# A two-block transformer kernel: the fourth sum of each pair of down weights, made by an adding DMA before, made by VectorE

## The reference, cut to what matters

```python
def conv_gated_ffn(x, w_up, w_gate, conv_w, conv_b, w_down):
    u = x @ w_up
    g = causal_dwconv(x @ w_gate, conv_w, conv_b)
    return (jax.nn.silu(g) * u) @ w_down

def swiglu(h, w_gate, w_up, w_down):
    return (jax.nn.silu(h @ w_gate) * (h @ w_up)) @ w_down
```

## Time and profile before

| what | value |
|---|---|
| median of 3 runs | 2264.41 us (2259.07 to 2270.99) |
| the profiled execution's own time | 2263.4 us |
| its span in the profile | 2261.8 us |
| TensorE's granted clock, mean | 0.997 of full |
| VectorE, ScalarE, GpSimd busy | 73%, 53%, 32% of the span |
| transfers | 350.75 MB, 155 GB/s in the mean |
| queue of GpSimd's transfers | 92.29 MB, 19.3% of 16 engines |

### The profile page before, as it was taken

The page is one execution under the profiler, slowest core; times in us unless marked ns, Lnnn a source line. Parts: engine busy times, 40 slices in busy tenths (PEclk is TensorE's granted clock), DMA queues, the critical chain, the costliest instruction groups (busy, mean ns, idle before and its releaser), DMA issues.

```text
span 2261.8 us, 37043 instructions
## 1 busy us (share of the span) xinstructions
PE 2195.7 (97%) x13094; PEld 1886.0 (83%) x13094; DVE 1644.0 (73%) x2447; ACT 1199.5 (53%) x2126; POOL 720.7 (32%) x482
## 2 busy tenths in 40 slices
PE   8999999999999999999999999999899999999998
PEld 6767898888888787899987899988778768899986
DVE  6966656678744345766698888888658972899898
ACT  6665444456655545443465644456645674444475
POOL 6944444321236535322102322221112343311101
PEclk9999999999999999999999999999999999999999
DMA  6636465675458864332264256695354593223364
GB/s 207 197 117 246 147 154 140 152 209 192 159 198 170 193 237 139 118 102 97 98 214 163 75 139 145 144 244 189 136 190 150 123 148 93 101 96 110 102 223 144
DMA packets 117497, 350.75 MB, mean 155 GB/s; under 512 B 12496, under 2 KB 12496, under 8 KB 117328
## 3 DMA queue, kind: packets, MB, share of 16 engines
q1 hardware_dynamic: 76320, 242.91, 32.0%
q0 software_dynamic: 36928, 92.29, 19.3%
q10 hardware_dynamic: 4144, 14.16, 1.9%
HBM read 338.76 MB, written 94.37 MB: 191 GB/s over the span
## 4 chain that ended last, share of the span: by engine, by line
PE 75%; DVE 10%; ACT 6%; DMA 5%; issue 2%; POOL 1%; DVEq 0%; SPq 0%; ACTq 0%; POOLq 0%
PE banks L953 9%; PE banks L955 8%; PE banks L954 8%; PE banks L1162 5%; PE banks L1164 5%; PE banks L1163 5%; PE banks L1251 4%; PE banks L1253 4%; PE banks L1252 4%; DMA raw<-ws 4%; PE banks L1296 3%; PE banks L1298 3%; PE banks L1297 3%; PE banks L986 2%; PE banks L988 2%
## 5 line engine op out<-in xcount | busy, mean ns | idle before, releaser
L1849 ACT ACTIVATE wH<-raw 128x1024 fp32r<-128x1024 f32 x363 | 380.9, 1052 | 419.3 <-DMA raw<-ws 138.5
L690 POOL TENSOR_TENSOR wL<-raw,wH 128x1024 fp32r<-128x1024 f32 x110 | 282.4, 2572 | 447.5 <-ACT wH L1849 444.0
L953 PE MATMUL banks<-xH,wH 128*128 128x512 f32 (+1 forms) x1080 | 413.4, 383 | 11.4 <-DVE xL L2587 7.4
L954 PE MATMUL banks<-xL,wH 128*128 128x512 f32 (+1 forms) x1080 | 407.8, 378 | 0.0
L955 PE MATMUL banks<-xH,wL 128*128 128x512 f32 (+1 forms) x1080 | 407.7, 377 | 0.0
L953 PEld LDWEIGHTS banks<-xH,wH 128*128 128x128 f32 x1080 | 203.7, 189 | 57.0 <-DVE wL L2592 8.5
L955 PEld LDWEIGHTS banks<-xH,wL 128*128 128x128 f32 x1080 | 203.6, 188 | 38.0
L954 PEld LDWEIGHTS banks<-xL,wH 128*128 128x128 f32 x1080 | 203.9, 189 | 35.4
L853 POOL TENSOR_TENSOR wL<-raw,wH 128x1024 fp32r<-128x1024 f32 x36 | 100.6, 2796 | 187.0 <-ACT wH L1849 187.0
L1162 PE MATMUL banks<-wH,mixXH 128*128 128x512 f32 x312 | 122.8, 393 | 12.0 <-DVE mixXL L2996 7.0
L1163 PE MATMUL banks<-wH,mixXL 128*128 128x512 f32 x312 | 121.5, 389 | 0.0
(11 more groups left out here) (416 smaller groups left out, 6230.4 us busy)
## 6 DMA issues: line engine op xcount, KB each, us to landing
raw<-ws SPq DMA_DIRECT2D x327, 512.0 KB, 3.3
raw<-sums SPq DMA_DIRECT2D x44, 512.0 KB, 4.2
sums<-ws POOLq DMA_DIRECT2D x20, 1024.0 KB, 6.4
firsts<-ws POOLq DMA_DIRECT2D x44, 256.0 KB, 5.0
sums<-firsts POOLq DMA_DIRECT2D x44, 256.0 KB, 5.8
thirds<-ws POOLq DMA_DIRECT2D x44, 256.0 KB, 6.3
sums<-sums POOLq DMA_DIRECT2D x44, 256.0 KB, 5.7
raw<-ws SPq DMA_DIRECT2D x44, 256.0 KB, 3.3
```

Of the source, the lines that this page charges most:

```text
L690: pool.tensor_tensor(wL[:, j, :], raw[:, j, :], fp(wH[:, j, :]), ALU.subtract).then_inc(low_ready, 1)
L953: pe.matmul(bank, wH[:, slot, cols], rh, start=start, stop=False)
L954: pe.matmul(bank, wH[:, slot, cols], rl, start=False, stop=False)
L1849: act.activation(high_slot(c)[:, 0:w], raw_slot(c)[:, 0:w], ACT.Copy).then_inc(high_ready, 1)
```

## The change: what it does, and the diff

The adding transfer of the fourth sum is removed from GpSimd's list, in every place where it stood, with the semaphore `fourth_added` and SyncE's wait for it. The row of `sums` that SyncE loads into the slot of an odd chunk now has the bare quarter in its left half. VectorE adds the right half to the left in the slot (`fourth_sum` in VectorE's list), once the load has landed, and ScalarE's high part of an odd chunk waits for that (`fourth_there`, semaphore `fourth_made`). The addition for pair 0 stands in the last tile of gate-and-up, ahead of `part_sums(0)`; that for pair 1 right after `low_of_chunk(0)`; that for pair p + 1 between the low parts of h of pair p and `low_of_chunk(2p + 1)`. The step-wise sums have one step less.

```diff
                     elif i < FT:
                         sp_e.wait_ge(second_added, 16 * n + 16)
-                        sp_e.wait_ge(fourth_added, 16 * n + 16)
                         sp_e.dma_start(to, sums[n]).then_inc(loaded(c), 16)
...
-            def fourth_sum(inst, j, t=0):
-
-                n = NP * inst + j
-                pool.wait_ge(second_added, t * 16 + (16 * n + 16))
-                if n:
-                    pool.wait_ge(fourth_added, t * 16 + 16 * n)
-                pool.sem_inc(adding, 1)
-                pool.dma_start(half_of(sums, t + n, 0), half_of(sums, t + n, 1), accum_op=ALU.add)\
-                    .then_inc(fourth_added, 16)
-
...
                 if 1 <= j <= NP:
                     second_sum(inst, j - 1)
-                if j >= 2:
-                    fourth_sum(inst, j - 2)
...
                     first_sum(inst, 2, t)
-                    fourth_sum(inst, 1, t)
                     low(cp + 9, t)
...
+                def fourth_there(j):
+                    act.wait_ge(fourth_made, NP * inst + j + 1)
+
...
                     if last:
+                        fourth_there(0)
                         high(d0 + 1)
...
                     def chunk(i):
+                        if i < FT and i % 2:
+                            fourth_there(i // 2)
                         high(d0 + i, w=S if i == Y_AT[NP - 1] else D)
...
                     if last:
+                        fourth_sum(0)
                         part_sums(0)
                         low_of_chunk(1)
...
+                def fourth_sum(j):
+                    c = d0 + 2 * j + 1
+                    dve.wait_ge(loaded(c), 16 * LOADED[c])
+                    quarters = raw_slot(c)
+                    dve.tensor_tensor(quarters[:, 0:S], quarters[:, 0:S], quarters[:, S:D], ALU.add).then_inc(fourth_made, 1)
...
                     low_of_chunk(0)
+                    fourth_sum(1)
...
                         parts(p, 2 * p)
+                        if p + 1 < NP:
+                            fourth_sum(p + 1)
                         low_of_chunk(2 * p + 1)
```

More of the change, by code:

```diff
@@ L366, in build_block @@
         third_added = sem("third_added")
-        fourth_added = sem("fourth_added")
+        fourth_made = sem("fourth_made")
         adding = sem("adding")
@@ L830, in plain_splits @@
                         first_sum(inst, 0, t)
-                        fourth_sum(inst, -1, t)
                         low_of_last_sum(u, 1, t)
@@ L838, in plain_splits @@
                     first_sum(inst, count - 1)
-                    fourth_sum(inst, count - 2)
                     low_of_last_sum(u, 1, count - 1)
@@ L844, in plain_splits @@
                         first_sum(inst, j)
-                        fourth_sum(inst, j - 1)
                         second_sum(inst, j)
                         third_sum(inst, j)
-                    fourth_sum(inst, NP - 1)
                     return
@@ L874, in plain_splits @@
                 first_sum(inst, 1)
-                fourth_sum(inst, 0)
                 low(cp + 5)
@@ L890, in plain_splits @@
                         first_sum(inst, j + 1)
-                    fourth_sum(inst, j)
             def down_parts(inst):
@@ L920, in _ @@
                 if inst == 1:
-                    for n in range(NP + 2):
+                    for n in range(NP + 1):
                         split(begun // SLOTS, begun % SLOTS)
```

## The result

The changed kernel takes **2270.55 us** (median of 20 runs, 2266.96 to 2274.58), the kernel before, run beside it, 2264.14 (20 runs): a ratio of **1.0027, 95% interval 1.0019 to 1.0035**. That is inside the range and within 0.5%, so "same" was right, and 5 us above the forecast of 2265.4; the rise is 6.4 us where 2.0 was forecast. The profiled execution took 2269.18 us with a span of 2267.5.

The account below looks back on a forecast made before the run. TensorE was taken as the bound, busy 2195.7 of 2261.8 us. Down stages +5.0 less 3.0 in gate-and-up gave +2.0 on the profiled 2263.4: 2265.4 us, range 2256 to 2274.

Parts of the forecast that it names:

- Pairs of 4.94 us, additions of 0.69: Down stages: a VectorE addition takes 0.69 us and lengthens its pair from 4.34 to 4.94, under TensorE's 5.44.
- Starts of instances 0 and 1, +1.0 each: Start of these down stages: the first two additions delay TensorE by 0.44 and 0.60 us, with no wait for a load.
- Instance 3, a new wait at the head of VectorE's queue, +1.6: Down stage start: the second addition waits for chunk 3, costing 1.35 us; the third, for chunk 5, another 0.3.
- Instance 2, +1.4 between -2.5 and +3.3: Down stage start: +3.3 us with the same landings, -2.5 with landings as in instance 3; a third of the way taken.
- From the third pair on the additions cost nothing: Down stages: VectorE's lead still grows by 0.50 us a pair instead of 1.10, so later additions stay covered.
- rival 3: Inside the pairs: additions lengthened beside GpSimd's tensor work make VectorE the bound, 16 us more, 2281; chance 0.05.
- Gate-and-up, -2.5 and -0.5: Gate-and-up of instances 2 and 0: less adding traffic shortens TensorE's waits of 5.7 and 1.8 us by 2.5 and 0.5.
- Rival 1, no relief: Other adding transfers remain in flight, no load comes sooner, down stage starts cost 8.1 us: 2271.5; chance 0.20.

Follow-up runs that it names:

- combines_off: Changed kernel with GpSimd's three additions of kept parts in each down stage left out of the computation: 2264.75 us, ratio 0.9996.
- traffic_back: Changed kernel plus a fourth adding transfer per pair, issued by GpSimd into a scratch tensor that nothing reads: 2279.38 us, ratio 1.0075.
- split_late_first: Changed kernel, adding transfers back in instances 1 and 3, pair 1's addition behind its low parts, instance 0's kept-part additions on VectorE: 2263.20 us, ratio 0.9987.
- gpsimd_sum: Changed kernel with the 44 additions of quarters made by GpSimd in the down stage instead of VectorE: 2298.95 us, ratio 1.0149.
- before_combine: Kernel before, adding transfers kept, with the three additions of kept parts in each down stage on VectorE instead of GpSimd: 2261.60 us, ratio 0.9998.
- late_first: Changed kernel with only pair 1's addition moved, from ahead of its part sums to behind its low parts: 2271.19 us, ratio 1.0028.

## Why the prediction was right, and where it wasn't

- **Pairs of 4.94 us, additions of 0.69.** Right: 44 of 685 ns in the mean, and successive pairs begin 4.94 apart, here in DVE's timeline:

```profile
519.38 0.68 DVE L2952 TENSOR_TENSOR raw<-raw 128x512 f32<-128x512 f32 x1
...
524.32 0.69 DVE L2952 TENSOR_TENSOR raw<-raw 128x512 f32<-128x512 f32 x1
```

- **Starts of instances 0 and 1, +1.0 each.** Right: TensorE's first wait went from 0.63 to 1.04 in both, the third from 0.50 and 0.53 to 1.12 and 1.10. No wait for a landing in either.
- **Instance 3, a new wait at the head of VectorE's queue, +1.6.** Right: 1.1 us of waiting for chunk 3 were forecast, and the stage grew by 1.8. In answer to the earlier trace rows (DVE, then PE):

```profile
2155.43 0.69 DVE L2952 TENSOR_TENSOR raw<-raw 128x512 f32<-128x512 f32 x1 [1.05 <-DMA raw<-sums]
...
2159.38 0.50 PE L1142 MATMUL banks<-wH,mixXH 128*128 128x512 f32 x1 [1.25 <-DVE mixXL L2994]
```

- **Instance 2, +1.4 between -2.5 and +3.3.** It was +2.1, by waits and clock together. VectorE waits 3.86 us for chunk 3 at its second addition and 1.63 for chunk 5 at its third, against the earlier trace rows:

```profile
1499.72 0.69 DVE L2952 TENSOR_TENSOR raw<-raw 128x512 f32<-128x512 f32 x1 [3.86 <-DMA raw<-sums]
...
1503.67 0.50 PE L1142 MATMUL banks<-wH,mixXH 128*128 128x512 f32 x1 [4.06 <-DVE mixXL L2994]
...
1505.25 0.69 DVE L2952 TENSOR_TENSOR raw<-raw 128x512 f32<-128x512 f32 x1 [1.63 <-DMA raw<-sums]
```

  The waits at the start sum to hardly more than before (5.28 us start to start against 5.00), but now one of them is 4.45 us long, and half clock follows it.
- **"From the third pair on the additions cost nothing."** This is the step that failed. It holds for the pairs, to whose end I followed it: no matmul waits there. But a lead that grows by 0.50 instead of 1.10 is 0.60 x 9 = 5.4 us shorter when the pairs are over, and behind the pairs stand GpSimd's three operations. I had the price of such contention in rival 3 and dismissed it with "within the pairs GpSimd has no tensor work to do"; true, and the wrong place to look. The row of 7.0 us shown above, TensorE's wait for VectorE near the end of all four stages, said already before the change that VectorE's time counts there. The contention cost 2.7 and 4.3 us in instances 0 and 1 (111.7 and 112.9 against combines_off's 109.0 and 108.6), of which 1.7 and 3 are half clock in this one trace.
- **Gate-and-up, -2.5 and -0.5.** Right in kind, too small in size. Over the traces here instance 2's stage takes 184.7 to 186.7 us (mean 185.8) in eleven kernels without the fourth transfer under it, and 189.7, 191.2, 190.4 in three with it: -4.7. Instance 0's takes 198.5 to 199.5 (mean 198.9) against 201.8, 200.6, 200.6: -2.1. I sized it by TensorE's waits, 5.7 and 1.8, and took half of them or less; the whole of them was nearer. The loads that VectorE waits for show why, but they aren't the size either: in instance 0, 6.4 us less of such waits went with 3.3 us less of the stage.
- **Rival 1, no relief.** It fell: loads do come sooner with one adding transfer fewer, though three remain (7.4 us of waits to 1.0, back to 5.0 with the transfer). The rule of the Trainium skill, page "DMA: Bandwidth & Descriptors", section on queues, rings and completion order, led me to it only with the assumption that the adding queue always holds something where it hurts. The traces speak against that assumption, not against the rule: by their DMA packets, that queue has something in flight in 90 of the 202 us of instance 0's gate-and-up stage before, in 74 of 199 in the changed kernel and in 89 of 201 in traffic_back.
- **The number.** Forecast +5.0 - 3.0 = +2.0, found +13 - 7 = +6. That the forecast was near is luck: two terms of opposite sign were too small by similar factors, 2.6 and 2.3. The range carried it.

**Open:** why 2.13 us of waiting lowers the clock in one trace and not in the next, and what that costs in a typical execution; whether bytes or GpSimd's issues make the relief; 2 us of traffic_back; and whether split_late_first is faster at all.

## What to carry to other kernels

An engine's lead over its consumer is a store, and "hidden" work spends it: follow it to the next place where it is needed, not to the end of the loop that you change. There, look at what else runs at that moment: here a VectorE operation beside a GpSimd one lasted until the other's end, and moving GpSimd's work onto the late engine made that engine earlier. Work that is moved to another engine also stands behind that engine's list, as the 19.7 us of gpsimd_sum show. And to judge lighter traffic, read beside the last engine's waits what the waited-for engine itself waits for.

## What the runs showed of the hardware

- A VectorE tensor_tensor of 0.42 us took 1.52 beside a GpSimd tensor_tensor of 128x512 (1.34 and 1.53 us). Others, of 0.42 to 1.22 us alone, took 1.4 to 2.9 beside one of 128x1024 (2.4 to 2.9). The same 128x1024 operation takes VectorE 1.16 us in a row of three.
- In these traces the clock fell to its lower level for 3 to 7 us within a few us behind single waits of TensorE of 2.1 to 4.9 us. 2.13 us did it in before_combine and not in the kernel before; 3.10 did it at the end of instance 1's stage in late_first and not in instance 0's. Such a stage then takes 1.6 to 3 us more, in one trace and not in another with the same wait, so a stage's length in one trace is good to about that.
- ScalarE's load of an activation table took 1.28 us, and VectorE stood 1.23 us for the operation behind it.
